# Two sets of transposes moved from TensorE to VectorE's 32x32 blocks and transfers, and two groups of small products moved to other steps

## The reference

```python
for l in range(DEPTH):
    h = rms_norm(x, norm_mix[l])
    proj = h @ w_in[l]
    (dq, dk, dv, dz, da, db, mq, mk, mv, lx, ly, gates) = split_columns(proj)
    y_dn = gated_deltanet(dq, dk, dv, dz, da, db, ...) @ dn_out[l]
    y_mb = moba_attention(mq, mk, mv) @ mb_out[l]
    y_lru = rg_lru_branch(lx, ly, ...) @ lru_out[l]
    g = jax.nn.sigmoid((gates + b_gate[l]).astype(jnp.float32)).reshape(b, t, N_BRANCH, d)
    mixed = (g[:, :, 0] * y_dn + g[:, :, 1] * y_mb + g[:, :, 2] * y_lru).astype(x.dtype)
    x = x + mixed @ w_o[l]
    h = rms_norm(x, norm_ffn[l])
    gate, up = jnp.split(h @ ffn_in[l], 2, axis=-1)
    x = x + (jax.nn.silu(gate) * up) @ ffn_down[l]
return rms_norm(x, norm_final)
```

## Time and profile before

| | |
|---|---|
| Median of three runs | 912.84 us |
| Profiled execution | 913.46 us |
| Its span in the profile | 911.7 us |
| Time around the span | 1.8 us |
| TensorE's granted clock, mean | 0.998 |
| DMA engines' busy share | 57.4% in SP's queue |

### The profile page before, as it was taken

One profiled execution on the slowest core, in us unless ns is written; L12 is line 12 of the kernel. 1 busy time (PEld: TensorE's weight loads), 2 busy tenths in 40 slices (PEclk: granted clock), 3 DMA queues, 4 the chain that ended last, 5 costly groups with the idle time before them and its releaser, 6 DMA issues.

```text
span 911.7 us, 13902 instructions
## 1 busy us (share of the span) xinstructions
PE 900.4 (99%) x5476; PEld 768.0 (84%) x5476; DVE 659.9 (72%) x1092; ACT 513.4 (56%) x877; POOL 2.4 (0%) x6
## 2 busy tenths in 40 slices
PE   9999999999999999999999999999999999999996
PEld 5999899788888888888879998988888888888885
DVE  6869876797867666656688797767977675665756
ACT  6587555875436444445475766568644554444443
POOL 0000000000000000000000000000000000000000
PEclk9999999999999999999999999999999999999999
DMA  8644434456554667777745344255655467767761
GB/s 295 203 162 162 143 113 159 159 196 234 178 196 162 212 201 246 215 217 250 218 169 179 117 162 134 99 185 185 228 195 185 154 214 207 249 206 235 233 203 46
DMA packets 89777, 171.13 MB, mean 188 GB/s; under 512 B 44656, under 2 KB 49520, under 8 KB 89712
## 3 DMA queue, kind: packets, MB, share of 16 engines
q1 hardware_dynamic: 89424, 170.16, 57.4%
q10 hardware_dynamic: 288, 0.08, 0.0%
HBM read 164.44 MB, written 5.77 MB: 187 GB/s over the span
## 4 chain that ended last, share of the span: by engine, by line
PE 94%; DVE 3%; ACT 1%; issue 0%; DVEq 0%; ACTq 0%
PE bank L532 7%; PE bank L434 7%; PE bank L435 7%; PE bank L436 7%; PE bank L533 7%; PE bank L534 7%; PE bank L609 6%; PE bank L337 5%; PE bank L338 5%; PE bank L339 5%; PE bank L377 5%; PE bank L376 5%; PE bank L378 5%; PE bank L365 2%; PE bank L364 2%; PE bank L366 2%
## 5 line engine op out<-in xcount | busy, mean ns | idle before, releaser
L869 ACT CAST whi<-raw 128x1024 fp32r<-128x1024 f32 x292 | 305.6, 1053 | 301.6 <-PE bank L436 92.9
L1206 DVE TENSOR_TENSOR wlo<-raw,whi 128x1024 fp32r<-128x1024 f32 x292 | 350.7, 1217 | 73.4 <-ACT whi L869 71.0
L337 PE MATMUL bank<-ahi,whi 128*128 128x256 f32 x448 | 129.6, 289 | 0.8 <-DVE tmp L1256 0.8
L338 PE MATMUL bank<-alo,whi 128*128 128x256 f32 x448 | 126.6, 283 | 0.0
L339 PE MATMUL bank<-ahi,wlo 128*128 128x256 f32 x448 | 126.6, 283 | 0.0
L532 PE MATMUL bank<-whi,ahi 128*128 128x512 f32 x288 | 114.4, 397 | 1.3 <-DVE small L1288 0.8
L534 PE MATMUL bank<-whi,alo 128*128 128x512 f32 x288 | 112.3, 390 | 0.0
L434 PE MATMUL bank<-whi,ahi 128*128 128x512 f32 x288 | 112.2, 390 | 0.0
L533 PE MATMUL bank<-wlo,ahi 128*128 128x512 f32 x288 | 112.2, 390 | 0.0
L436 PE MATMUL bank<-whi,alo 128*128 128x512 f32 x288 | 112.1, 389 | 0.0
L435 PE MATMUL bank<-wlo,ahi 128*128 128x512 f32 x288 | 112.0, 389 | 0.0
(11 more groups left out here) (267 smaller groups left out, 1304.2 us busy)
## 6 DMA issues: line engine op xcount, KB each, us to landing
raw<-stream_dram SPq DMA_DIRECT2D x292, 512.0 KB, 4.5
turned_dram<-proj SPq DMA_DIRECT2D x144, 32.0 KB, 1.7
proj<-turned_dram SPq DMA_DIRECT2D x18, 256.0 KB, 4.5
proj<-gbias_dram SPq DMA_DIRECT2D x12, 256.0 KB, 4.2
par<-params_dram SPq DMA_DIRECT2D x2, 556.5 KB, 7.5
x<-x_dram SPq DMA_DIRECT2D x2, 512.0 KB, 5.2
out_dram<-x SPq DMA_DIRECT2D x4, 256.0 KB, 2.3
con<-consts_dram SPq DMA_DIRECT2D x1, 612.0 KB, 5.5
```

What stands on the lines that cost most here:

```text
L337: pe.matmul(dst, whi_of(m)[:, wcol], hi, start=first, stop=False, skip_group_check=True)
L338: pe.matmul(dst, whi_of(m)[:, wcol], lo, start=False, stop=False, skip_group_check=True)
L869: act.copy(whi_of(m), raw_of(m)).then_inc(*AC.up(("hi", m), "w"))
L1206: dv.tensor_tensor(wlo_of(m), raw_of(m), whi_of(m), ALU.subtract).then_inc(*DV.up(("lo", m), "w"))
```

## The change

In each of the two layers:

- **Probabilities.** The 12 transposes on TensorE and their three copies on ScalarE are gone. At step 36 VectorE transposes within 32x32 blocks (three instructions of 128x512), then SP at its step 40, before it loads half 45, writes them to DRAM with four DMAs, waits for them, and reads all back turned. `pv` waits for that read.
- **Places.** `qs` moves from k = 34 to 35, `pv` from 37 to 40, `wi` from 40 to 42, `wr` from 42 to 44; ScalarE's and VectorE's steps of the recurrence each move by two, `mb_out` from 39 to 42, the bias load of gate group 0 from SP's step 41 to 40.
- **Mixture, first half.** The 8 transposes on TensorE are gone. VectorE transposes within blocks at step 66 (two of 128x512), SP at step 70 writes with eight DMAs, waits, and reads 512 KB back; ScalarE and VectorE round and split it at step 70.

The core of the diff:

```diff
         SQJ, XS = 52, 36
         PR, PT, VTOK = 48, 54, 8
-        S1, WB, VN0, VN1, O1, OJ, OZ, ZT = 36, 16, 18, 38, 20, 8, 4, 4
+        S1, WB, VN0, VN1, O1, OJ, OZ, ZT = 36, 16, 18, 38, 20, 24, 4, 4
         XC, TR, TI, A0, UU, HS = 12, 8, 0, 24, 20, 12
+        MIX32, MIXT = 36, 44
         MIX, GB = 0, (16, 18)
         JUNK, FINAL, XW = 44, TZ, 8
...
 
         def mix_turned(hf, i):
-            return bank[(4, 0)[hf] + i]
+            return bank[i][:, :] if hf else flat(tiles(MIXT + 2 * i, 2))
...
+                    if k == 40:
+                        sp.wait_ge(*DV.at(l, "probs32"))
+                        for a in range(4):
+                            sp.dma_start(probs.rearrange("b c (g q) -> c g b q", q=P)[:, :, :, 32 * a:32 * a + 32],
+                                         flat(tiles(PT, 6, slice(32 * a, 32 * a + 32))).rearrange("c (g b k) -> c g b k", g=12, b=4)
+                                         ).then_inc(written_probs, 16)
+                        sp.wait_ge(written_probs, 64 * (l + 1))
+                        sp.dma_start(flat(tiles(PR, 6)), probs.rearrange("b c n -> (b c) n")).then_inc(loaded_probs, 16)
+                    if k == 70:
+                        for t in range(2):
+                            sp.wait_ge(*DV.at(l, ("mix32", t)))
+                            for a in range(4):
+                                sp.dma_start(mixture[:, :, t * P + 32 * a:t * P + 32 * a + 32].rearrange("b c r -> c b r"),
+                                             flat(tiles(MIX32 + 2 * t, 2, slice(32 * a, 32 * a + 32))).rearrange("c (b r) -> c b r", r=32)).then_inc(written_mix, 16)
+                        sp.wait_ge(written_mix, 128 * (l + 1))
+                        sp.dma_start(tiles(MIXT, 4), mixture.rearrange("(f b) c t -> (b c) f t", f=4)).then_inc(loaded_mix, 16)
                     if l * NH + k + RING < NM:
                         load(l * NH + k + RING)
                     for e in range(6):
-                        if k == (GATE0 + 5, GATE0 + 2)[e] if e < 2 else k == GATE0 + 4 * e + 1:
+                        if k == (GATE0 + 4, GATE0 + 2)[e] if e < 2 else k == GATE0 + 4 * e + 1:
                             sp.wait_ge(*(DV.at(l, ("gate", e - 2, 1)) if e > 1 else PE.at(l, "o0" if e else ("vn", 1))))
                             sp.dma_start(flat(tiles(GB[e % 2], 2)), gbias[l, e]).then_inc(loaded_gb[e % 2], 16)
...
-                if k == 35:
-                    pe.wait_ge(*DV.at(l, "probs"))
-                    pe.wait_ge(*AC.at(l, "state"))
-                    pr = flat(tiles(PR, 6))
-                    for g in range(12):
-                        ins = pe.transpose(b3((2, 3, 5)[g // 4], 4)[:, g % 4, :], pr[:, g * P:(g + 1) * P], ident[:, :])
-                    ins.then_inc(*PE.up("pT"))
-                if k == 37:
-                    pe.wait_ge(*AC.at(l, "pcopy"))
-                    vt, pt = wide(VTOK, 4), wide(PT, 6)
+                if k == 40:
+                    pe.wait_ge(loaded_probs, 16 * (l + 1))
+                    pe.wait_ge(*DV.at(l, "masked"))
+                    vt, pt = wide(VTOK, 4), wide(PR, 6)
                     for h in range(HEADS):
...
+                if k == 35:
                     for h in range(HEADS):
                         ins = exact(b3(6, 4)[:, h, :], proj[:, TQ + h, P:T], wide(S1, 2)[:, h, :])
...
-                if k in (40, 42):
-                    w = "wi" if k == 40 else "wr"
-                    if k == 40:
+                if k in (42, 44):
+                    w = "wi" if k == 42 else "wr"
+                    if k == 42:
                         pe.wait_ge(*DV.at(l, ("xc", 1)))
                         pe.wait_ge(*DV.at(l, "mb_out"))
                     else:
...
                         y_half(l, k, y_bank(i))
-                        if i == 3 and half:
-                            turn_mixed(l, 0)
...
-                if k == 36:
-                    act.wait_ge(*PE.at(l, "pT"))
-                    for i in range(3):
-                        act.copy(flat(tiles(PT + 2 * i, 2)), bank[(2, 3, 5)[i]][:, :]).then_inc(*AC.up("pcopy"))
-                if k == 38:
+                if k == 41:
                     act.wait_ge(*PE.at(l, "pv"))
                     for i in range(2):
                         act.copy(flat(bhi[:, 4 + 2 * i:6 + 2 * i, :]), bank[2 + i][:, :]).then_inc(*AC.up())
...
-                if k in (41, 43):
-                    w, dst, bias = ("wi", TI, "bih") if k == 41 else ("wr", TR, "brh")
...
-                if k == 44:
+                if k == 46:
...
-                if k in (68, 74):
-                    hf = (k - 68) // 6
-                    act.wait_ge(*PE.at(l, ("mixT", hf)))
+                if k in (70, 74):
+                    hf = int(k == 74)
+                    if hf:
+                        act.wait_ge(*PE.at(l, ("mixT", 1)))
+                    else:
+                        act.wait_ge(loaded_mix, 16 * (l + 1))
                     for i in range(2):
                         q = 2 * hf + i
-                        act.activation(flat(ahi[:, 2 * q:2 * q + 2, :]), mix_turned(hf, i)[:, :], ACT.Copy, scale=0.5).then_inc(*AC.up(("mixhi", q)))
...
+                if k == 36:
+                    dv.wait_ge(*DV.at(l, "probs"))
+                    for i in range(3):
+                        step(dv.transpose(flat(tiles(PT + 2 * i, 2)), flat(tiles(PR + 2 * i, 2))), "probs32")
...
-                if k == 39:
+                if k == 42:
                     dv.wait_ge(*AC.at(l, "mbhi"))
                     for i in range(2):
                         step(dv.tensor_tensor(flat(blo[:, 4 + 2 * i:6 + 2 * i, :]), bank[2 + i][:, :],
...
-                if k == 43:
+                if k == 45:
                     dv.wait_ge(*AC.at(l, "tanh_i"))
                     step(dv.scalar_tensor_tensor(out=tiles(TI, 4), in0=tiles(TI, 4), scalar=1.0, in1=tiles(XC, 4),
                                                  op0=ALU.add, op1=ALU.mult))
...
                     dv.wait_ge(*PE.at(l, ("bulk", k - 1)))
                     dv.wait_ge(*AC.at(l, ("gate", e)))
+                    dv.wait_ge(*DV.at(l, "lru_out"))
...
                             settle(1)
                             step(dv.tensor_tensor(mix_tiles(t, hf), mix_tiles(t, hf), gate_tiles(e, t), ALU.add), ("mixf", hf, t))
-                if k in (68, 74):
-                    hf = (k - 68) // 6
+                            if hf == 0 and br == 2:
+                                settle()
+                                step(dv.transpose(flat(tiles(MIX32 + 2 * t, 2)), mix_tiles(t, 0)), ("mix32", t))
+                if k in (70, 74):
+                    hf = int(k == 74)
                     for i in range(2):
                         q = 2 * hf + i
                         dv.wait_ge(*AC.at(l, ("mixhi", q)))
-                        step(dv.scalar_tensor_tensor(out=flat(alo[:, 2 * q:2 * q + 2, :]), in0=mix_turned(hf, i)[:, :], scalar=0.5,
+                        step(dv.scalar_tensor_tensor(out=flat(alo[:, 2 * q:2 * q + 2, :]), in0=mix_turned(hf, i), scalar=0.5,
                                                      in1=flat(ahi[:, 2 * q:2 * q + 2, :]).bitcast(F32), op0=ALU.mult, op1=ALU.subtract),
                              ("mixed", q))
...
+        args.append(nc.dram_tensor("mixture_dram", (16, 32, T), F32, kind="Internal").ap())
         args.append(nc.dram_tensor("turned_dram", (2, 8, 32, T), F32, kind="Internal").ap())
+        args.append(nc.dram_tensor("probs_dram", (4, 32, 12 * P), F32, kind="Internal").ap())
```

More of the change, by code:

```diff
@@ L97, in last, with build @@
         return self.sem, self.n - back
-def build(nc, wstream, params, gbias, consts, norms, final, x_in, ident_in, ab_in, turned, out, known):
+def build(nc, wstream, params, gbias, consts, norms, final, x_in, ident_in, ab_in, mixture, turned, probs, out, known):
     ctx = ExitStack()
@@ L141, in build @@
         stored = sem("stored")
+        written_mix, loaded_mix = sem("written_mix"), sem("loaded_mix")
         written_hid, loaded_hid = sem("written_hid"), sem("loaded_hid")
+        written_probs, loaded_probs = sem("written_probs"), sem("loaded_probs")
         PE = Signal(sem("tensor_done"), "pe", known)
@@ L1061, in side @@
                     act.copy(flat(tiles(VN1, 2)), bank[7][:, :]).then_inc(*AC.up(("vn", 1)))
-                if k in (41, 43):
-                    w, dst, bias = ("wi", TI, "bih") if k == 41 else ("wr", TR, "brh")
+                if k in (43, 45):
+                    w, dst, bias = ("wi", TI, "bih") if k == 43 else ("wr", TR, "brh")
                     act.wait_ge(*PE.at(l, w))
@@ L1071, in side @@
                                            bias=sm[bias][pa, t:t + 1], scale=0.5).then_inc(*AC.up())
-                    AC.mark("tanh_i" if k == 41 else "tanh_r")
+                    AC.mark("tanh_i" if k == 43 else "tanh_r")
                 if k == 39:
@@ L1086, in side @@
```

(22 more changed lines are left out.)

1 line of the change is left out of this document (added).

## The result

The changed kernel takes 915.96 us, the median of ten runs (915.06 to 916.85); the kernel before, in the same stretch of runs, takes 912.87 (912.35 to 913.72). The ratio is 1.0032, with a 95% interval of 1.0024 to 1.0040: slower by 3.1 us. Forecast was 910.9. The time lies inside the forecast's range, on the side that I held less likely than the faster one.

What follows compares the result with a forecast made beforehand. TensorE, busy 99% of the span, was taken as the bound: 1.94 us shed less 1.0 us of waiting per layer, over two layers 1.9 us, so the median becomes 910.9; range 908.4 to 919.

Steps and rivals of the forecast that it cites:

- what TensorE sheds: Transposes removed and groups moved on TensorE: 1.94 us less per layer, 3.9 us for two layers.
- when TensorE arrives: End of half 40 comes at 159.50, where `pv` wants the probabilities; `wi` wants `mb_out` at 167.84.
- the pace of the pieces: The probabilities' 128-byte pieces are written at 169 GB/s, so 786 KB take 4.65 us.
- R: Time when SP issues the read of the probabilities: 149.15 + 0.35 + 4.65 + 1.50 = 155.65.
- the term of 0.35: Delay of the probabilities' writes by the load of half 44 queued ahead: up to 1.1 us, taken as 0.35.
- the bias at R + 6.0: Bias of gate group 0, behind the read and the load of half 45, lands at R + 6.0 = 161.65.
- T: TensorE's loss per layer at `pv` or `wi`, whichever is later: R - 154.65, put at 1.0 us.
- the mixture: The mixture's transfer is ready at 249.5, half 72 starts at 251.0: 1.5 us to spare, no cost.
- Rival 2: Long runs of short pieces at two thirds of the burst's pace, 7.0 us: T = 3.3, 915.6, chance 0.20.
- Rival 3: Each short piece of the writes costs double, 9.3 us: T = 5.65, 920.3, chance 0.11.
- Rival 4: Issue of the writes grows with pieces, 11.4 us, and the mixture costs 2.2 more: 928, chance 0.12.
- Rival 1: Nothing waits, the read issued under 154.65 or the bias earlier: 908.9, chance 0.22.

Runs made afterwards that it cites:

- e3: Changed kernel without the probabilities' writes and read; `pv` waits only for VectorE's transposes, attention values not the reference's: 910.14 us.
- e1: Kernel before with only the mixture's first half turned by VectorE's blocks and a transfer, probabilities, `pv` and gates as before: 911.80 us.
- e8: e7 with the bias of gate group 0 also loaded ahead of the probabilities' writes: 909.82 us.
- e6: Changed kernel with the probabilities' writes ahead of the load of half 44, which now stands behind their read: 919.54 us.
- e2: Changed kernel without its mixture part, the mixture turned on TensorE again: 916.63 us.
- e7: Changed kernel with `pv` at 42, `wi` at 44, `wr` at 46 and dependent ScalarE and VectorE steps two halves later, same transfer: 911.81 us.
- e5: Changed kernel with the bias of gate group 0 loaded at SP's step 39, ahead of the probabilities' writes: 917.19 us.
- e4: Changed kernel writing the same probabilities' bytes in four DMAs of long rows, 128 pieces instead of 6144, attention values not the reference's: 910.44 us.

## Why the prediction was wrong, point by point

**Right: what bounds the kernel. Nearly right: what TensorE sheds.** 3.9 us were forecast. The 3.7 that TensorE is busy less look like it, but by luck: 0.58 of them are the opening. The better measure is e3, where nothing waits between `ks` and half 68. TensorE's lead over the kernel before grows there from 0.49 (138.77 for 139.26) to 2.65 (238.61 for 241.26), by 2.2 us for the 1.94 forecast. That is a little more than worked out, and it is not kept.

**Left out: the layer's end.** A gain upstream is not a gain at the end. e1 has 0.15 of its 0.90 us left at the next layer. In e3 TensorE's lead falls from 2.70 to 1.25 at the layer's end, and in e8 from 3.09 to 1.45; 1.1 and 1.2 of that are the waits in the lists, most of the rest are slower starts behind the waits. A hidden tile that comes by transfer holds up the last tile's steps on ScalarE and VectorE, and this transfer does not move up with TensorE. In the changed kernel the same place takes 0.67. I had looked for new waits only near the change.

**Right: when TensorE arrives, the issue of the writes, the pace of the pieces.** Half 40 ended at 159.56 for 159.50. The four writes took 4.31 and 4.51 to issue for "about 4". Short pieces went at 163 GB/s in the changed kernel and at 176 in e6, against 169.

**Wrong: R, by the term of 0.35.** This is the step that failed first. The read was issued at 156.67, or 157.24 on the forecast's clock, instead of 155.65. The phase had 4.65 + 1.50 for the writes by themselves and 0.35 for what is ahead of them. Measured were 8.23 and 7.70, so 2.1 and 1.6 stand where the 0.35 did. e6 shows that 0.3 of it is there with nothing ahead, so the load of half 44 costs 1.2 to 1.7 more in this execution. I had bounded it at 1.1 in all by halving fixed parts of a landing, and then took a third of the bound, without a row. A bound that holds is the load's landing itself: issued 1.8 us ahead of the first write and landing at the median 4.7 behind its issue (the page, part 6), it could hold the engines until 2.9 us into the phase. What is ahead orders the phases: 6.5 and 6.5 with nothing (e6), 6.8 to 8.2 with a load (e2, e7, the changed kernel), 8.1 to 9.2 with a load and a bias (e5, e8). The spread within one queue is in part the tail of few bytes, for which the forecast had no term.

**Wrong: the bias at R + 6.0.** It came at R + 7.0 in the first layer and R + 6.6 in the second (611.93 less 605.29). I counted the three transfers up to it; SP issues more loads at once behind, and 1.89 MB moved before it had landed.

**Right in form: T.** The wait at `pv` and the one at `wi` add up to one lateness, as worked out: 1.90 + 1.45 = 3.35 in the first layer, 1.38 + 1.08 = 2.46 in the second, against 1.0. The forecast's working, 0.8 before rounding, with 1.6 more from R and 1.0 more from the bias makes 3.4. The 1.90 at `pv` are these 1.6 and 0.3 of the read, which landed 4.2 behind its issue for 3.9. Over both layers T is 5.8 us for the forecast's 2.0. These 3.8 put the forecast of 910.9 at 914.7, the layer's end at about 915.4; measured were 915.96. The decision point of T = 1.94 per layer shows how thin the forecast was: the two terms together had to hold to 0.9 us, and I gave the read no slack at all in the sum. So a gain of 1.9 us was forecast and a loss of 3.1 came. The forecast named the wait at `wi` and put "none or little" at `pv`, which became the longer one.

**Right: the mixture.** Its writes go from 239.42 to 245.03, a phase of 5.6 for 5.0; half 72 did not wait.

**The rivals.** Rival 2 named the price, T = 3.3 and 915.6, but that is luck: its mechanism was another, short pieces at two thirds of the pace. e6 refutes that, its pieces go at 176 GB/s. Rival 3, each short piece costing double, would have made the phase 11 us, and did not come. Short pieces are slow all the same, 163 to 176 GB/s against 331, and the phase with long rows (e4, a load ahead) is shorter than the one with short pieces and nothing ahead (e6), 4.7 to 4.85 against 6.5. The Trainium skill, page DMA: Bandwidth & Descriptors, section Specifications, puts line rate at pieces of 512 bytes or more. The runs agree that pieces of 128 bytes are below it; they have no pieces near 512 and can't show where the limit lies. The price was in the burst's pace already, and nothing came on top of it. Rival 4, issue by pieces: 4.3 and not 11.4. Rival 1 is what e8 has, by other means: nothing waits there.

## What to carry to other kernels

A transfer that takes the place of work on the engine that bounds the kernel is a chain of queue positions. Bound what is in flight ahead of it by the whole landing time that is left, and price what follows it by all bytes that are issued before the consumer's own have landed. Where the sum's margin is under a microsecond, as here, move the consumers later if their buffers allow it: here that was worth about 4 us in the medians (e7), and 6.1 with the bias ahead of the writes (e8), which is 2.9 faster than before. Put a small transfer that a second chain needs ahead of the large one only if the large one has slack (e5 lost by it, e8 won by it). Look for the next transfer-bound place downstream, where a gain can be given back. And before two profiles are compared, compare a place ahead of the change: here the traces differ by up to 0.9 us at `ks`.

## What the hardware showed that I had not expected

A long wait cost more than itself. Around idle stretches of 2.98, 3.00 and 2.46 us TensorE's granted clock went to its lower level, 0.50, for somewhat over 3 us (0.64 to 0.80 are means of stretches with both levels), and the products in it took 1.99 for 1.09 and 4.57 for 2.95. Against the changed kernel and with the opening taken out, TensorE is busy 1.5 us more in e5, which has one such stretch, and 2.8 more in e6, which has two. It comes in every execution of the two kernels: their mean granted clock is 0.996 in all five runs of e5 and 0.993 to 0.995 in those of e6, and 0.997 to 0.999 in the ten of the changed kernel. Behind the changed kernel's 1.90, 1.45, 1.38 and 1.08, the 1.96 of e5 and the 2.17 of e4 it stayed at 1.00, as in this stretch of the changed kernel behind its longest wait:

```profile
161.00:164.00 3.00, 3.00 (x26) 1.00 0.92 317
```

That is three cases in two kernels against six in three; no run was made to vary the wait by itself.
